# Expert blocks of a mixture layer: the next block's rows are transposed behind the down products, and their first half signals on its own

## The chip, the cores and the metric

The kernel runs on one core of a Trainium2 chip. The metric is the device time of one execution in microseconds, as the median of several runs; lower is better. The engines are TensorE (PE), VectorE (DVE), ScalarE (ACT), GpSimd (POOL) and SyncE (SP). Each has its own instruction queue and works through it in order; they wait for each other by semaphores.

## The reference, cut to what matters

One step of a two-layer decoder for 1024 prompt rows and 8 sample rows of 1024 columns, all in f32. Each layer has a mixer, a layer norm, a mixture of experts and a layer norm. The change lies in the mixture of experts:

```python
vals, idx = lax.top_k(jnp.where(in_group, probs, -1.0), TOP_K)      # 2 of 16 experts for each row
...
for e in range(N_EXPERTS):
    h = jax.nn.silu(xt @ w_gate[e]) * (xt @ w_up[e])                # 1024 -> 256
    y = y + dense_gate[:, e:e + 1] * (h @ w_down[e])                # 256 -> 1024
x = layer_norm(ALPHA * x + f)
```

## The kernel before

`experts` is called once for each of the two layers. It first works out which rows go to which expert and lays them out in half blocks of 64 rows: a half block belongs to one expert. Two half blocks make a block of 128 rows. Then `steps` runs `body(i, u, first)` on every engine for each block j = 2i + u, up to the last one in use. Buffers with index u alternate from block to block.

Of a block, the low half (columns 0 to 63 of the turned rows) is multiplied with weights straight from the ring of four experts' weights (`wgu`, `wd`), and the high half with a copy of its expert's weights (`half_wgu`, `half_wd`, both in `x_rows`), which VectorE and ScalarE make anew for each block. The two products of a pair run in the two column halves of TensorE's array.

The engines' orders in `body` for block j:

- **TensorE.** Waits for the turned rows' two halves (`xca`, `xcv`) and for both parts of the copied gate/up weights (`b_gate_up` at 2j + 2). Gate/up products for k = 0 to 7 (L2432, L2433) into bank 2 + u. Then `transpose_x`: eight transposes (L2405) of the rows of block j + 1 into banks 0 and 1, signal `xt` after the last. Then `down` of block j - 1 (L2417, L2418) into banks 5 and 6. Then two transposes (L2447) of block j's hidden into bank 4, signal `ht`. In the first block of a stage there are no down products.
- **VectorE.** `second_half(j + 1, ..., 0)`: copies part 0 of the gate/up weights of the next block's second half (L2651), once that expert's weights are `loaded` and TensorE is through the fourth gate/up pair (`b_read`). Then the product of silu and up (L2661, signal `h`). Then `copy_x`: the high half of the turned rows out of bank 1 (L2482, signal `xcv`), after `xt`. Then part 1 of the weights (L2651 again, signal `b_gate_up`). Then `out` of block j - 1: y = alpha x + down products (L2645), signal `y`.
- **ScalarE.** `second_half(j - 1)`: down weights of the second half (L2498, `b_down`). Alpha times x (L2507, `alpha_x`). Silu (L2511). `copy_x` of the low half (L2482, `xca`), after `xt`. `out(j - 1)`: store of y by a DMA (L2489), after `y`. Then the copy of the transposed hidden (L2516, `hc`), after `ht`; the down products of block j wait for `hc`.
- **GpSimd.** `load_rows`: the gather of the rows of block j + 1 by an indirect DMA (L2368, L2371), after `xt` and `alpha_x` of the block before.
- **SyncE.** Loads an expert's weights (three DMAs of 1 MB, L2243 and L2245) once the down products of the expert that had the set are through (`halves_plus_1`), waits until they have landed, signals `loaded` (L2347), and goes on to the next expert.

Of the kernel before, what the change touches and what calls it, by code (L numbers as in the profile page):

```python
# [35 lines left out]
P = 128  # L36
# [2220 lines left out]
def experts(nc, io, layer, xr, lg, gates, slots, table, weights, tables, stored, const, ahead, s_ahead):  # L2257
# [7 lines left out]
    with Memory(nc, f"ex{layer}") as m:  # L2265
        wgu, wd, s_w = weights
        p = m.sb("probs", [P, TILES, E])
# [32 lines left out]
        pb = m.psum("pb", [P, 8, 512])  # L2300

        r = {k: m.sem(f"route_{k}") for k in "mx ex as rk chain lanes blocks sum parts part tokens token_list now tokens_set tab".split()}
        q = {k: m.sem(k) for k in "gu xt halves_plus_1 ht silu h xca xcv hc alpha_x y b_read b_gate_up b_down loaded stored".split()}
        s_xs = [m.sem(f"x_rows{u}") for u in range(2)]
        s_st = m.sem("y_rows_stored")
        s_last = m.sem("x_rows_of_last_landed")
# [91 lines left out]
        @block.tensor  # L2398
        def _(pe):
            mm = nc.tensor.matmul  # L2400

            def transpose_x(i, u):
                pe.wait_ge(s_xs[u], 16 * i + 16)
                for k in range(KD):
                    last = nc.tensor.transpose(pb[:, k // 4, P * (k % 4):P * (k % 4) + P], xs[:, u, P * k:P * k + P],  # L2405
                                            const["ident"][:, :])
                last.then_inc(q["xt"], 1)

            def down(j, c):

                w = wd[:, bass.ds(c, 1), :, :].rearrange("p c k n -> p (c k) n")
                pe.wait_ge(q["b_down"], j + 1)
                pe.wait_ge(q["hc"], j + 1)
                for half in range(2):
                    cols = slice(512 * half, 512 * half + 512)
                    for k in range(2):
                        a = mm(pb[0:HALF, 5 + half, :], hT[:, k, 0:HALF], w[:, k, cols], start=(k == 0), stop=(k == 1))  # L2417
                        b = mm(pb[HALF:P, 5 + half, :], hT[:, k, HALF:P], half_wd[:, k, cols], start=(k == 0), stop=(k == 1))  # L2418
                a.then_inc(q["halves_plus_1"], 1)
                b.then_inc(q["halves_plus_1"], 1)  # L2420

            def body(i, u, first):
                j = 2 * i + u
                c = entry(pe, j, 0, E - 1) % SETS
                w = wgu[:, bass.ds(c, 1), :, :].rearrange("p c k n -> p (c k) n")
                pe.wait_ge(q["xca"], j + 1)
                pe.wait_ge(q["xcv"], j + 1)
                pe.wait_ge(q["b_gate_up"], 2 * j + 2)
                if not first:
                    pe.wait_ge(q["h"], j - 1)  # L2430
                for k in range(KD):
                    mm(pb[0:HALF, 2 + u, :], xT[:, k, 0:HALF], w[:, k, :], start=(k == 0), stop=(k == KD - 1))  # L2432
                    last = mm(pb[HALF:P, 2 + u, :], xT[:, k, HALF:P], half_wgu[:, k, :], start=(k == 0), stop=(k == KD - 1))  # L2433
                    if k == 3:
                        last.then_inc(q["b_read"], 1)
                last.then_inc(q["gu"], 1)
                transpose_x(i + u, 1 - u)
                if not (first and u == 0):
                    c_before = entry(pe, j - 1, 0, E - 1) % SETS
                    if not first:  # L2440
                        pe.wait_ge(q["y"], j - 1)
                    down(j - 1, c_before)
                pe.wait_ge(q["h"], j + 1)
                if not (first and u == 0):
                    pe.wait_ge(q["hc"], j)
                for k in range(2):
                    last = nc.tensor.transpose(pb[:, 4, P * k:P * k + P], h[:, u, P * k:P * k + P], const["ident"][:, :])  # L2447
                last.then_inc(q["ht"], 1)
            a = A[:, :, :].rearrange("p t e -> p (t e)")
            pe.wait_ge(tables.sem, tables.all)  # L2450
            keep_busy(nc, pb[:, 1, :], const["ident"], 28)
            pe.wait_ge(r["as"], 1)
            mm(pb[:, 5, 0:TILES * E], t["ones"][:, :], A[:, :, :].rearrange("p t e -> p e t"), start=True, stop=True)
            mm(pb[:, 6, 0:TILES * E], t["not_earlier"][:, :], a, start=True, stop=True).then_inc(r["rk"], 1)
            keep_busy(nc, pb[:, 1, :], const["ident"], 28)
            pe.wait_ge(r["blocks"], 1)
            for c in range(2):
                pe.wait_ge(r["lanes"], c + 1)
                for i in range(TILES):
                    j = TILES * c + i  # L2460
                    g = RW * (j % RG)
                    last = mm(pb[g:g + RW, 7, 0:P], in_block[0:rows(i), c, i, :], at_lane[c][0:rows(i), i, :],
                              start=(j < RG), stop=(j + RG >= 2 * TILES))
            last.then_inc(r["parts"], 1)
            pe.wait_ge(r["sum"], 2)
            pe.wait_ge(r["part"], 1)
            mm(pb[:, 4, 0:NBLK], part, group_sum[:, 0:NBLK], start=True, stop=True).then_inc(r["tokens"], 1)
            transpose_x(0, 0)
            keep_busy(nc, pb[:, 2, :], const["ident"], 24)
            pe.wait_ge(r["tab"], 1)  # L2470

            pe.sem_inc(q["halves_plus_1"], 1)
            final = steps(pe, body)
            c = entry(pe, final, 0, E - 1) % SETS
            pe.wait_ge(q["y"], final)
            down(final, c)

        def copy_x(eng, copy, half, sem, j):

            eng.wait_ge(q["xt"], j + 1)  # L2480

            copy(xT[:, 4 * half:4 * half + 4, :], pb[:, half, :].rearrange("p (k t) -> p k t", k=4)).then_inc(q[sem], 1)  # L2482

        @block.scalar
        def _(act):
            def out(j):

                act.wait_ge(q["y"], j + 1)
                act.dma_start(io["slots_out"][bass.ds(j * P, P), :], y[:, :]).then_inc(s_st, 16)  # L2489

            def second_half(j, first):

                expert = entry(act, T_HALVES + j, 0, E - 1)
                act.wait_ge(q["loaded"], expert + 1)
                if not first:
                    act.wait_ge(q["halves_plus_1"], 2 * j + 1)
                src = wd[:, bass.ds(expert % SETS, 1), :, :].rearrange("p c k n -> p (c k n)")
                nc.scalar.copy(half_wd.rearrange("p k n -> p (k n)"), src).then_inc(q["b_down"], 1)  # L2498

            def body(i, u, first):  # L2500
                j = 2 * i + u
                if not (first and u == 0):
                    second_half(j - 1, first)
                act.wait_ge(s_xs[u], 16 * i + 16)
                if not first:
                    act.wait_ge(q["y"], j - 1)
                nc.scalar.activation(ax[:, u, :], xs[:, u, :], ACT.Identity, scale=ALPHA).then_inc(q["alpha_x"], 1)  # L2507
                act.wait_ge(q["gu"], j + 1)
                if not first:
                    act.wait_ge(q["ht"], j - 1)  # L2510
                nc.scalar.activation(h[:, u, :], pb[:, 2 + u, 0:FF], ACT.Silu).then_inc(q["silu"], 1)  # L2511
                copy_x(act, nc.scalar.copy, 0, "xca", j + 1)
                if not (first and u == 0):
                    out(j - 1)
                act.wait_ge(q["ht"], j + 1)
                nc.scalar.copy(hT[:, :, :], pb[:, 4, 0:2 * P].rearrange("p (k t) -> p k t", k=2)).then_inc(q["hc"], 1)  # L2516
            act.wait_ge(r["mx"], 1)
            nc.scalar.activation(p[:, :, :], p[:, :, :], ACT.Exp).then_inc(r["ex"], 1)
            act.wait_ge(r["parts"], 1)
            nc.scalar.copy(part, pb[0:RG * RW, 7, 0:P]).then_inc(r["part"], 1)  # L2520
            copy_x(act, nc.scalar.copy, 0, "xca", 0)
            act.wait_ge(r["tab"], 1)
            expert = entry(act, T_HALVES, 0, E - 1)
            act.wait_ge(s_stored, n_stored)
            act.wait_ge(q["loaded"], expert + 1)
            nc.scalar.copy(half_wgu[:, 0:4, :].rearrange("p k n -> p (k n)"),
                           wgu[:, bass.ds(expert % SETS, 1), 0:4, :].rearrange("p c k n -> p (c k n)")).then_inc(q["b_gate_up"], 1)
            last = steps(act, body)
            second_half(last, False)
            out(last)  # L2530
            act.wait_ge(s_st, 16 * last + 16)
            act.sem_inc(q["stored"], 1)
# [384 lines left out]
```

## Time and profile before

| what | value |
|---|---|
| median of 3 runs | 1544.02 us (1543.89 to 1549.71) |
| the profiled execution | 1542.83 us |
| its span, first to last instruction | 1541.0 us |
| TensorE busy | 1384.9 us (90%) |
| VectorE busy | 737.4 us (48%) |
| ScalarE busy | 443.1 us (29%) |
| mean granted TensorE clock | 0.943 of full |
| gate/up products (L2432 and L2433 side by side) | 279.8 us |
| down products (L2417 and L2418 side by side) | 148.3 us |

The profile is of one execution. The two expert stages lie at about 787 to 1052 us and 1210 to 1483 us of the span. A busy share is a mean over stages with different limits, so what the change is worth has to be read inside the expert stages. Matmuls are pipelined: the busy times of two that run side by side overlap, and the start of one to the start of the next tells how long a product takes.

### The profile page before, as it was taken

To read this page: it belongs to the slowest core of one execution; us is meant where nothing else is said; L and a number is where in the kernel's file an instruction comes from. 1 tells how busy PE (TensorE), PEld (TensorE's weight loads), DVE (VectorE), ACT (ScalarE), POOL (GpSimd) and SP (SyncE) were. 2 spreads that over 40 slices of the span, in tenths; PEclk is the share of its full clock that TensorE was granted. 3 is DMA by queue.
4 is the path that set the end of the run, shared out by engine and by line. 5 is a ranking of instruction groups with operands and counts; after the bars stand their busy time and mean duration, and the time that the engine had idled before them with its cause. 6 is when DMAs were issued, how large, how long until landed. Compare 5 with 4: busy or idle time off the path is not lost. (4 is left out here: it accounts for less than half of the span.)

```text
span 1541.0 us, 28066 instructions
## 1 busy us (share of the span) xinstructions
PE 1384.9 (90%) x11029; PEld 812.2 (53%) x11030; DVE 737.4 (48%) x1097; ACT 443.1 (29%) x804; POOL 209.9 (14%) x257
## 2 busy tenths in 40 slices
PE   6999999998789988999879999973998799999856
PEld 4666666665688874555553333322797533333212
DVE  1004444467467753867543333333884433333218
ACT  1004456432323321211113333321321223333311
POOL 4000000000434412110000110104100000100031
PEclk8999999999799998999989999995998899999978
DMA  8593000000300013000477788874204777886445
GB/s 216 98 368 90 2 28 28 28 1 4 72 20 4 5 31 121 28 28 29 166 269 249 276 299 292 283 237 163 97 21 176 271 251 254 287 305 241 175 163 207
DMA packets 135338, 226.76 MB, mean 147 GB/s; under 512 B 21970, under 2 KB 100803, under 8 KB 134954
## 3 DMA queue, kind: packets, MB, share of 16 engines
q1 hardware_dynamic: 114434, 151.13, 30.6%
q0 software_dynamic: 15184, 53.67, 9.5%
q10 hardware_dynamic: 5616, 20.45, 3.3%
q8 instruction: 79, 1.29, 0.3%
q14 instruction: 25, 0.20, 0.0%
HBM read 176.42 MB, written 50.35 MB: 147 GB/s over the span
## 5 line engine op out<-in xcount | busy, mean ns | idle before, releaser
L2432 PE MATMUL ex_pb<-ew_w_gate_up,ex_xT 128*64 x624 | 279.8, 602 | 7.8 <-DVE x_rows L2651 7.8
L2433 PE MATMUL ex_pb<-x_rows,ex_xT 128*64 128x512 f32 x624 | 279.8, 602 | 0.0
L518 PE MATMUL pj_pb<-pj_xT,pj_w 128*128 128x348 f32 (+1 forms) x912 | 275.5, 458 | 0.8 <-ACT pj_xT L553 0.8
L518 PEld LDWEIGHTS pj_pb<-pj_xT,pj_w 128*128 128x128 f32 x912 | 170.1, 189 | 94.7 <-issue 5.7
L2651 DVE COPY x_rows<-ew_w_gate_up 128x2048 f32 x80 | 97.8, 1222 | 174.6 <-PE ex_pb L2433 90.2
L2432 PEld LDWEIGHTS ex_pb<-ew_w_gate_up,ex_xT 128*64 128x64 f32 x624 | 83.1, 138 | 173.4 <-issue 173.1
L2417 PE MATMUL ex_pb<-ew_w_down,ex_hiddenT 128*64 x312 | 148.3, 620 | 11.8 <-ACT x_rows L2498 11.8
L2418 PE MATMUL ex_pb<-x_rows,ex_hiddenT 128*64 128x512 f32 x312 | 148.3, 620 | 0.0
L2417 PEld LDWEIGHTS ex_pb<-ew_w_down,ex_hiddenT 128*64 128x64 f32 x312 | 40.8, 141 | 89.1 <-issue 89.1
L2498 ACT COPY x_rows<-ew_w_down 128x2048 f32 x39 | 74.1, 1899 | 31.8 <-issue 29.6
L2433 PEld LDWEIGHTS ex_pb<-x_rows,ex_xT 128*64 128x64 f32 x624 | 83.1, 138 | 0.0
L829 DVE SCALAR_TENSOR_TENSOR mixed<-pj_pb,v_mu,mixed 128x347 f32<-128x347 f32 (+1 forms) x42 | 24.0, 572 | 106.4 <-ACT mixed L674 106.3
L2645 DVE TENSOR_TENSOR ex_y_rows<-ex_x_rows,ex_pb 128x1024 f32<-128x1024 f32 x37 | 45.1, 1220 | 61.8 <-PE ex_pb L2418 61.8
L2516 ACT COPY ex_hiddenT<-ex_pb 128x256 f32<-128x256 f32 x39 | 14.5, 373 | 197.2 <-DVE ex_y_rows L2645 197.2
L2368 POOL COPY ex_tokens_now<-ex_token_of_slot 128x1 uint32 (+1 forms) x41 | 10.1, 247 | 438.9 <-ACT ex_x_rows L2507 389.1
L674 ACT ACTIVATE mixed<-pj_pb,pj_one_minus_mu 128x347 f32<-128x347 f32 (+1 forms) x42 | 23.0, 548 | 149.0 <-PE pj_pb L518 149.0
L2004 PE MATMUL mo_pb<-late_rows,projected_qkv 128*128 128x512 f32 x128 | 60.3, 615 | 0.0
L2405 PEld LDWEIGHTS ex_pb<-k_ident,ex_x_rows 128*128 128x128 f32 x328 | 36.6, 145 | 43.4 <-issue 31.6
L2004 PE MATMUL mo_pb<-mo_w,minus_kk_then_y 128*128 128x512 f32 x128 | 58.0, 593 | 0.0
L2405 PE MATMUL ex_pb<-k_ident,ex_x_rows 128*128 128x128 f32 x328 | 46.6, 287 | 11.5 <-DMA ex_x_rows<-scratch_x_stored,ex_tokens_now 11.5
L2661 DVE TENSOR_TENSOR ex_hidden<-ex_hidden,ex_pb 128x256 f32<-128x256 f32 x39 | 16.4, 420 | 73.2 <-ACT ex_hidden L2511 73.2
L2733 PE MATMUL cb_pb<-cb_expert_rows,cb_gate_diagonals 128*128 128x512 f32 (+1 forms) x72 | 34.2, 623 | 16.0 <-DMA cb_expert_rows<-scratch_slots_out,slots 13.2
(431 smaller groups left out, 2248.6 us busy)
## 6 DMA issues: line engine op xcount, KB each, us to landing
ew_w_gate_up<-in_w_ex_gate SPq DMA_DIRECT2D x32, 1024.0 KB, 6.1
ew_w_gate_up<-in_w_ex_up SPq DMA_DIRECT2D x32, 1024.0 KB, 10.0
ew_w_down<-in_w_ex_down SPq DMA_DIRECT2D x32, 1024.0 KB, 12.5
scratch_slots_out<-ex_y_rows ACTq DMA_DIRECT2D x39, 512.0 KB
scratch_slots_out<-pj_tmp POOLq DMA_DIRECT2D x3, 4096.0 KB, 21.7
scratch_x_stored<-x_rows SPq DMA_DIRECT2D x16, 512.0 KB
pj_w<-in_w_in SPq DMA_DIRECT2D x7, 1024.0 KB, 9.7
minus_kk_then_y<-in_x_prompt SPq DMA_DIRECT2D x8, 512.0 KB, 5.9
```

The costliest lines, as they stand in the source:

```text
L518: last = nc.tensor.matmul(product(at)[:, 0:tn], w[:, k_slab % NW, k, c0:c0 + mrows], xT[:, k, x0:x0 + tn], start=(k == 0), stop=(k == KD - 1))
L829: last = stt(out=out[:, 0:n_prompt], in0=product(at)[:, 0:n_prompt], scalar=mu, in1=out[:, 0:n_prompt], op0=ALU.mult, op1=ALU.add)
L2004: last = mm(pb[0:n, 2 * (i % 2) + h, :], lhs(k, i), (w[:, k, 512 * h:512 * h + 512] if k < 4 else w_swa[:, k - 4, 512 * h:512 * h + 512]), ...
L2405: last = nc.tensor.transpose(pb[:, k // 4, P * (k % 4):P * (k % 4) + P], xs[:, u, P * k:P * k + P], const["ident"][:, :])
L2417: a = mm(pb[0:HALF, 5 + half, :], hT[:, k, 0:HALF], w[:, k, cols], start=(k == 0), stop=(k == 1))
L2418: b = mm(pb[HALF:P, 5 + half, :], hT[:, k, HALF:P], half_wd[:, k, cols], start=(k == 0), stop=(k == 1))
L2432: mm(pb[0:HALF, 2 + u, :], xT[:, k, 0:HALF], w[:, k, :], start=(k == 0), stop=(k == KD - 1))
L2433: last = mm(pb[HALF:P, 2 + u, :], xT[:, k, HALF:P], half_wgu[:, k, :], start=(k == 0), stop=(k == KD - 1))
L2498: nc.scalar.copy(half_wd.rearrange("p k n -> p (k n)"), src).then_inc(q["b_down"], 1)
L2645: nc.vector.tensor_tensor(y[:, :], ax[:, u, :], pb[:, 5:7, :].rearrange("p b n -> p (b n)"), ALU.add)\
L2651: nc.vector.tensor_copy(half_wgu[:, 4 * part:4 * part + 4, :].rearrange("p k n -> p (k n)"), src)\
L2733: last = nc.tensor.matmul(out[0:n, h, :], diag[0:n, i % 2, c, 0:n], r[0:n, i, c, half], start=(c == 0), stop=(c == 1))
```

## The change

Four edits, all in `experts`:

- On TensorE, `transpose_x` for block j + 1 moves from ahead of the down products of block j - 1 to behind them, so it stands right ahead of the transposes of hidden.
- The fourth transpose signals `xt_low`; the eighth signals `xt` as before. ScalarE's copy of the low half waits for `xt_low`, VectorE's of the high half for `xt`.
- On TensorE the wait for the high half (`xcv`) moves from ahead of the gate/up products to ahead of k = 4. The wait for `b_gate_up` stays.
- On ScalarE the copy of the transposed hidden moves ahead of `out(j - 1)`.

```diff
@@ transpose_x
                     last = nc.tensor.transpose(pb[:, k // 4, P * (k % 4):P * (k % 4) + P], xs[:, u, P * k:P * k + P],
                                             const["ident"][:, :])
+                    if k == 3:
+                        last.then_inc(q["xt_low"], 1)
                 last.then_inc(q["xt"], 1)
@@ body of TensorE
                 pe.wait_ge(q["xca"], j + 1)
-                pe.wait_ge(q["xcv"], j + 1)
                 pe.wait_ge(q["b_gate_up"], 2 * j + 2)
                 if not first:
                     pe.wait_ge(q["h"], j - 1)
                 for k in range(KD):
+                    if k == 4:
+                        pe.wait_ge(q["xcv"], j + 1)
...
                 last.then_inc(q["gu"], 1)
-                transpose_x(i + u, 1 - u)
                 if not (first and u == 0):
                     c_before = entry(pe, j - 1, 0, E - 1) % SETS
                     if not first:
                         pe.wait_ge(q["y"], j - 1)
                     down(j - 1, c_before)
+                transpose_x(i + u, 1 - u)
                 pe.wait_ge(q["h"], j + 1)
@@ copy_x
-            eng.wait_ge(q["xt"], j + 1)
+            eng.wait_ge(q["xt" if half else "xt_low"], j + 1)
@@ body of ScalarE
                 copy_x(act, nc.scalar.copy, 0, "xca", j + 1)
+                act.wait_ge(q["ht"], j + 1)
+                nc.scalar.copy(hT[:, :, :], pb[:, 4, 0:2 * P].rearrange("p (k t) -> p k t", k=2)).then_inc(q["hc"], 1)
                 if not (first and u == 0):
                     out(j - 1)
-                act.wait_ge(q["ht"], j + 1)
-                nc.scalar.copy(hT[:, :, :], pb[:, 4, 0:2 * P].rearrange("p (k t) -> p k t", k=2)).then_inc(q["hc"], 1)
```

## Rows read from the trace of the kernel before

**Rows 1.** The page, its costliest groups: one instruction of this line a block.
```profile
L2516 ACT COPY ex_hiddenT<-ex_pb 128x256 f32<-128x256 f32 x39 | 14.5, 373 | 197.2 <-DVE ex_y_rows L2645 197.2
```

**Rows 2.** Busy times by stretch, from a block's first gate/up product to the next's.
```profile
core 0: us, PE busy (x) PEld busy (x) DVE busy (x) ACT busy (x) POOL busy (x), PEclk, DMA share, GB/s
895.50:907.50 12.00, 12.00 (x59) 4.33 (x58) 4.57 (x6) 4.20 (x5) 1.72 (x2) 1.00 0.84 303
907.50:919.90 12.40, 12.08 (x59) 4.33 (x59) 4.76 (x6) 4.20 (x5) 1.15 (x2) 1.00 0.91 311
919.90:933.70 13.80, 12.13 (x58) 4.41 (x58) 4.31 (x6) 4.20 (x5) 1.14 (x2) 1.00 0.82 286
...
811.57:823.56 11.99, 11.99 (x59) 4.41 (x59) 3.70 (x5) 2.80 (x4) 1.14 (x2) 1.00 0.39 137
...
993.70:1011.60 17.90, 12.37 (x59) 4.40 (x58) 4.54 (x6) 4.20 (x5) 1.14 (x2) 0.93 0.80 275
1011.60:1025.70 14.10, 14.08 (x58) 4.83 (x58) 4.52 (x6) 4.20 (x5) 1.68 (x2) 0.85 0.98 303
...
1423.50:1442.80 19.30, 12.39 (x60) 4.43 (x60) 4.76 (x6) 4.20 (x5) 1.15 (x2) 0.91 0.74 259
1442.80:1456.40 13.60, 13.60 (x60) 4.73 (x60) 4.48 (x6) 4.20 (x5) 1.92 (x2) 0.88 0.26 96
```

**Rows 3.** Timeline of TensorE in an undisturbed block: start us, us, engine, line, what.
```profile
902.54 1.09 PE L2405 MATMUL ex_pb<-k_ident,ex_x_rows 128*128 128x128 f32 x8
...
903.56 0.64 PE L2417 MATMUL ex_pb<-ew_w_down,ex_hiddenT 128*64 x1
...
907.15 0.44 PE L2447 MATMUL ex_pb<-k_ident,ex_hidden 128*128 128x128 f32 x2
...
907.51 0.64 PE L2432 MATMUL ex_pb<-ew_w_gate_up,ex_xT 128*64 x1
...
914.53 1.09 PE L2405 MATMUL ex_pb<-k_ident,ex_x_rows 128*128 128x128 f32 x8
```

**Rows 4.** The same timeline, ScalarE and VectorE beside it.
```profile
903.67 0.59 ACT L2482 COPY ex_xT<-ex_pb 128x512 f32<-128x512 f32 x1 [0.63 <-PE ex_pb L2405]
903.67 0.69 DVE L2482 COPY ex_xT<-ex_pb 128x512 f32<-128x512 f32 x1 [0.18 <-PE ex_pb L2405]
...
904.28 1.22 DVE L2651 COPY x_rows<-ew_w_gate_up 128x2048 f32 x1
...
907.47 1.22 DVE L2645 TENSOR_TENSOR ex_y_rows<-ex_x_rows,ex_pb 128x1024 f32<-128x1024 f32 x1 [1.98 <-PE ex_pb L2418]
...
909.24 0.37 ACT L2516 COPY ex_hiddenT<-ex_pb 128x256 f32<-128x256 f32 x1 [4.99 <-DVE ex_y_rows L2645]
```

**Rows 5.** Timeline, end of a stage's first block, which has no down products.
```profile
808.32 1.09 PE L2405 MATMUL ex_pb<-k_ident,ex_x_rows 128*128 128x128 f32 x8
...
809.33 0.44 PE L2447 MATMUL ex_pb<-k_ident,ex_hidden 128*128 128x128 f32 x2
...
809.45 0.69 DVE L2482 COPY ex_xT<-ex_pb 128x512 f32<-128x512 f32 x1 [0.18 <-PE ex_pb L2405]
...
810.05 1.22 DVE L2651 COPY x_rows<-ew_w_gate_up 128x2048 f32 x1
...
811.57 0.64 PE L2432 MATMUL ex_pb<-ew_w_gate_up,ex_xT 128*64 x1 [1.80 <-DVE x_rows L2651]
```

**Rows 6.** Timelines of SyncE's queue and VectorE: the last expert's weights, both stages.
```profile
993.61 0.38 SPq L2243 DMA_DIRECT2D ew_w_gate_up<-in_w_ex_gate  x1
...
1008.13 1.23 DVE L2651 COPY x_rows<-ew_w_gate_up 128x2048 f32 x1 [13.36 <-SPq L2347]
...
1423.39 0.38 SPq L2243 DMA_DIRECT2D ew_w_gate_up<-in_w_ex_gate  x1
...
1439.22 1.23 DVE L2651 COPY x_rows<-ew_w_gate_up 128x2048 f32 x1 [14.54 <-SPq L2347]
```

**Rows 7.** Timeline, end of the first expert stage.
```profile
1037.60 1.22 DVE L2645 TENSOR_TENSOR ex_y_rows<-ex_x_rows,ex_pb 128x1024 f32<-128x1024 f32 x1 [1.89 <-PE ex_pb L2418]
...
1043.96 1.11 PE L2417 MATMUL ex_pb<-ew_w_down,ex_hiddenT 128*64 x1 [6.16 <-ACT x_rows L2498]
```

More of the change, by code:

```diff
@@ L2302, in experts @@
         r = {k: m.sem(f"route_{k}") for k in "mx ex as rk chain lanes blocks sum parts part tokens token_list now tokens_set tab".split()}
-        q = {k: m.sem(k) for k in "gu xt halves_plus_1 ht silu h xca xcv hc alpha_x y b_read b_gate_up b_down loaded stored".split()}
+        q = {k: m.sem(k) for k in "gu xt_low xt halves_plus_1 ht silu h xca xcv hc alpha_x y b_read b_gate_up b_down loaded stored".split()}
         s_xs = [m.sem(f"x_rows{u}") for u in range(2)]
```

## Prediction

> **What bounds the kernel now.** I read the page first: the list of costliest groups says that the expert blocks are 39 in all, over the two expert stages [rows 1]. Then the table of stretches, one stretch a block, counted from the first gate/up product of a block to that of the next [rows 2]. The reader should see two kinds of row. In an undisturbed one (895.50 to 907.50) TensorE is busy for 12.00 of 12.00 us at granted clock 1.00, with VectorE at 4.57 and ScalarE at 4.20: the block is bound by TensorE and nothing else is near it. In the others TensorE was kept waiting, or ran at a lower clock.
>
> Third, the order on TensorE inside an undisturbed block [rows 3]. Gate/up at 907.51, transposes of the next rows at 914.53: 7.02 us for gate/up. The down products start 1.02 us after the transposes (902.54 to 903.56), the transposes of hidden 3.59 us after that (907.15), and the next gate/up 0.36 us later. 7.02 + 1.02 + 3.59 + 0.36 = 11.99 us. TensorE has no hole in it.
>
> Fourth, what the other engines do meanwhile [rows 4]. Both halves of the turned rows are copied at 903.67, 1.13 us after the transposes began. VectorE then copies the second part of the second half's gate/up weights (L2651, 904.28, 1.22 us), which ends at 905.50. The next gate/up needs the rows and both weight parts: `b_gate_up` is awaited in full at the top of the block. All of that is there at 905.50 and wanted at 907.51. The cover is the down products, and the spare time is 2.0 us.
>
> **The change part by part.** *The move of the eight transposes.* It removes no instruction. The down products now follow gate/up directly; I take 7.02 us for gate/up, as the wait, the table entry and the products replace the transposes at the same place, then 3.59 us to the end of the down products. Then come the transposes, at time T, and behind them only the transposes of hidden, 0.36 us, instead of 3.59 + 0.36.
>
> What is late next is VectorE's program order, which the diff leaves alone: copy of the high half of the turned rows (waits for all eight transposes), then L2651 (second weight part), then the next gate/up can start. The low half's own signal doesn't help this chain, nor does the later `xcv` wait on TensorE, since `b_gate_up` stays where it was and its second increment comes behind the high copy.
>
> The trace of before has exactly this order once per stage, in the first block, which has no down products [rows 5]: transposes at 808.32, hidden's at 809.33, VectorE's copy at 809.45, L2651 at 810.05, gate/up at 811.57 after 1.80 us of idle that is put down to L2651. From the transposes to gate/up: 3.25 us. I take it as it stands.
>
> New block: 7.02 + 3.59 + 3.25 = 13.86 us against 11.99: **+1.87 us a block**. It holds for each step from one gate/up to the next in which down products stood between: not for the first step of a stage, which had this order already. 39 blocks in two stages make 37 steps, less 2 is 35. 35 x 1.87 = **+65.4 us**, all of it on TensorE's path.
>
> *The signal after the fourth transpose.* ScalarE's copy of the low half can start earlier than 1.13 us after T. Nobody who is last waits for it: 0. The cover is VectorE's chain; without that, see the second rival. The extra increment and the wait for `xcv` ahead of the fifth product don't show in this trace. Bounds: 0 below (no data leaves the path), and above 0.1 us each, since a table entry and three waits between hidden's transposes and gate/up fit into 0.36 us together with two transposes [rows 3]; I take 0, the nearer to that row, and keep 35 x 0.1 = 3.5 us for the range.
>
> *ScalarE: hidden's copy ahead of `out`.* Before, the copy at 909.24 waited behind the store, which waited for y (907.47) [rows 4]. Now it runs at once, and behind it come the store, the down weights' copy and alpha times x. Who waits for it is the down product a whole gate/up later: 0 in the middle of a stage. POOL's queue waits for alpha x and the transposes; the rows it fetches are wanted a block later than they land, and that point moves later: 0. The store's DMA is issued some 2.5 us later in the block, in a block that grows by 1.87: 0.
>
> *y, and the tail of a stage.* VectorE's y (L2645) stands behind L2651. In the last block nothing covers this: y, store, down weights' copy, last down products. Before, y started at 1037.60 and the last down products at 1043.96, 6.36 us later [rows 7]; gate/up had begun at 1025.70 [rows 2], so 18.26 us in all. Now y starts when VectorE is through L2651: T + 1.73 for its start (808.32 to 810.05) and 1.13 for the following one, T + 2.86, with T 10.61 us after gate/up; then 6.36, less 0.39 for the hidden copy that no longer stands in between. 10.61 + 2.86 + 6.36 - 0.39 = 19.44: +1.2 us, twice: **+2.4 us**.
>
> *Waits for weights that go.* Six steps were longer than 11.99 us [rows 2]: 12.40, 13.80, 17.90, 14.10 (clock 0.85), 19.30, 13.60 (clock 0.88). Together 91.1 - 71.9 = 19.2 us lost. Two rows show the cause of the big ones [rows 6]: the last expert's load is issued at 993.61, when the down products free a set, and VectorE starts on it at 1008.13, 14.5 us later; in the second stage 1423.39 and 1439.22, 15.8 us. The issue stood 0.1 us ahead of gate/up; now the down products end 3.25 us ahead of gate/up, and the issue comes some 2.9 us ahead of it. The weights are there 11.6 and 12.9 us into the block, and gate/up follows 3.5 us after them as before (1008.13 to 1011.60): 15.1 and 16.4 us against 13.86, so 1.2 and 2.5 us remain. The two small waits (0.4 and 1.8 us) are shorter than what one block gives to the loads, and go. That TensorE ran at a lower clock came only with the two longest idles (17.90 less 12.37 and 19.30 less 12.39 us, so 5.5 and 6.9 us); what remains is 3.1 and 4.4 us with the 1.9 us, in pieces, so I let the cost of the clock go as well. **-(19.2 - 1.2 - 2.5) = -15.5 us**. If none of it comes back, 0; if all, -19.2.
>
> **Sum**, against the profiled execution's 1542.83 us: +65.4 + 2.4 - 15.5 = +52.3, 1595.1 us. The profiled run lies 1.2 us under the median of the runs (1544.02), so I say **1596 us** for a median, +3.4%.
>
> **Rivals.** *The clock falls in every block.* Each block now has about 1.9 us of idle TensorE. In the two steps at low clock, 2.1 and 1.6 us were lost [rows 2]; at 35 blocks x 1.85 that is +65 more, 1661 us. Against it: the same 1.80 us of idle stands ahead of 811.57 and the stretch behind it reads 1.00; the stretch of 13.80 us, with 1.7 us idle, reads 1.00 too [rows 2, 5]. For it: it would now recur every 13.9 us, which no row shows. Chance 5%. The Trainium skill, page "TensorE: Matmul & The Clock Gate", section "A second HAM failure mode: psum-queue depth-cycling", describes this: frequent short idles between groups of products make the clock go back and forth between its two levels.
>
> *The copies are all that is exposed, and the loads pay for it.* This is the case on the other side, not slower. It needs the second weight part to be in place ahead of the turned rows, or TensorE not to stand still for `b_gate_up`. Then gate/up waits for the low copy alone: fourth transpose done some 0.62 us after T (a little over half of the 1.09 us of the eight), 0.63 for ScalarE's copy, 0.30 from copy to product as at 811.27 to 811.57: T + 1.55 against T + 1.37, +0.18 us a block, 6.3 us. With the sets freed 1 us earlier, 5 to 9 of the 19.2 us come back: 1540 to 1544 (1542.8 + 6.3 + 1.2, less that). It decides at whether the 1.22 us copy of L2651 stands behind the high copy in VectorE's order; the code says so, and [rows 5] shows TensorE waiting for it. Chance 4%: 3% within half a per cent, 1% faster.
>
> *The price is paid, but no wait for weights shrinks*, because the late loads come from their own succession and not from the set's release: 1542.8 + 65.4 + 2.4 + 1.2 = 1612 us. For it: in the first stage the loads run back to back for long stretches. Against it: then 35 us more time would help them even more. Chance 15%.
>
> **How the numbers follow.** Forecast with its neighbourhood, 76%: 1587 to 1606 (0.1 us a block either way, 3.7 us of loads either way, 2.4 of tail). Rival without recovery 15%, clock 5%, covered 4%. The range for 8 in 10 goes from 1582 to 1614: it takes in the third rival, and for its lower end a block that costs 1.6 us instead of 1.87 with all 19.2 us given back (1542.8 + 56 + 2.4 - 19.2 + 1.2 = 1583). What measurement can tell from no change is about 0.5%, 8 us. Slower by over that: 96%; within: 3%; faster: 1%.
>
> **What would show it.** TensorE's gate/up group (L2432) gets an idle of about 1.9 us in 37 of 39 blocks, released by VectorE's L2651, some 65 us in total instead of 7.8; undisturbed blocks last 13.86 us; VectorE's high copy is released by the transposes and L2651 follows it by 0.6 us; the wait at the last expert's load shrinks from about 5.6 us to under 3; the clock in the middle of a stage stays 1.00. Wrong would be: gate/up released by ScalarE's copy or by nothing, a block near 12.2 us, or stretches well under 1.00.

## The result

| | before | after |
|---|---|---|
| median of the runs shown together | 1545.8 us (4 runs) | 1595.71 us (4 runs, 1594.8 to 1598.55) |
| ratio | | 1.0312, 95% interval 1.0273 to 1.0350 |
| profiled execution / its span | 1542.83 / 1541.0 us | 1598.55 / 1596.7 us |

The change makes the kernel slower by 3.1%. 1596 us was forecast, and 3.4% on the median then known.

The timeline of the changed kernel, one block in the middle of the first expert stage, is below (start us, us, engine, line, what). Its file has more lines, so the numbers have moved, and they move again in the kernels of the experiments: here L2419 are the down products, L2435 gate/up, L2450 hidden's transposes, L2485 the copies of the turned rows, L2654 the weights' copy, L2648 y.

```profile
902.93 0.59 PE L2419 MATMUL ex_pb<-ew_w_down,ex_hiddenT 128*64 x1
...
906.47 1.09 PE L2405 MATMUL ex_pb<-k_ident,ex_x_rows 128*128 128x128 f32 x8
907.16 0.59 ACT L2485 COPY ex_xT<-ex_pb 128x512 f32<-128x512 f32 x1 [3.63 <-PE ex_pb L2405]
...
907.40 0.38 PE L2450 MATMUL ex_pb<-k_ident,ex_hidden 128*128 128x128 f32 x2
907.60 0.69 DVE L2485 COPY ex_xT<-ex_pb 128x512 f32<-128x512 f32 x1 [3.62 <-PE ex_pb L2405]
...
908.21 1.22 DVE L2654 COPY x_rows<-ew_w_gate_up 128x2048 f32 x1
909.34 1.22 DVE L2648 TENSOR_TENSOR ex_y_rows<-ex_x_rows,ex_pb 128x1024 f32<-128x1024 f32 x1
909.71 0.64 PE L2435 MATMUL ex_pb<-ew_w_gate_up,ex_xT 128*64 x1 [1.93 <-DVE x_rows L2654]
...
916.62 0.59 PE L2419 MATMUL ex_pb<-ew_w_down,ex_hiddenT 128*64 x1
```

This is [rows 5] in every block. ScalarE's low half is copied by 907.75, VectorE's high half by 908.29, and gate/up still waits until L2654 is through at 909.43. In [rows 3, 4] the same copies ran under the down products. From gate/up to down products 6.91 us, to the transposes 3.54, to gate/up 3.24.

The waits of TensorE (us in total, times, longest), and the stretches from one gate/up to the next, columns as in [rows 2]:

```profile
PE ex_pb L2435 <- DVE x_rows L2654: 69.1, 37, 1.9
```

```profile
841.44:855.13 13.69, 11.76 (x59) 4.55 (x59) 4.69 (x6) 4.20 (x5) 1.14 (x2) 1.00 0.79 279
855.13:868.73 13.60, 11.76 (x58) 4.55 (x59) 4.52 (x6) 4.20 (x5) 1.14 (x2) 1.00 0.35 105
...
1480.33:1494.98 14.65, 11.98 (x59) 4.54 (x59) 4.51 (x6) 4.20 (x5) 1.15 (x2) 1.00 0.91 310
1494.98:1508.58 13.60, 11.76 (x58) 4.53 (x59) 4.51 (x6) 4.20 (x5) 1.15 (x2) 1.00 0.27 100
```

That is 69.1 us of waiting in 37 starts; before it was 7.8 us in 6. TensorE works 11.76 us of a block's 13.60 or 13.69; the two lengths alternate, 13.65 in the mean. The only block longer than that is the one at 1480.33, so of the six long stretches of [rows 2] one small one is left.

The next table shows where the 55.7 us between the two spans lie. The edges are the first gate/up product of an expert stage and the start of its last down products:

| stretch | before | after | difference |
|---|---|---|---|
| up to the first gate/up product | 801.3 | 803.9 | +2.6 |
| first expert stage | 242.7 | 262.3 | +19.6 |
| between the expert stages | 177.4 | 185.6 | +8.2 |
| second expert stage | 252.7 | 276.8 | +24.1 |
| to the end | 67.0 | 68.2 | +1.2 |

So 43.7 us are in the expert stages, and 12 outside them, where the change touches nothing. Most of those are one thing. In both traces TensorE stands still for 19.9 us behind the first expert stage, does 8.4 us of small products for the layer's mixer and stands still for 2.0 us more. The stretches below start behind that, first before, then after. The products come in the same order in both; at the lower clock fewer of them fit into a stretch.

```profile
1080.90:1085.00 4.10, 4.05 (x19) 3.50 (x20) 3.97 (x5) 0.43 (x1) 2.68 (x3) 0.60 1.01 393
1085.00:1090.00 5.00, 5.00 (x22) 1.36 (x22) 1.45 (x2) 1.81 (x3) 0.00 (x0) 1.00 0.72 285
```

```profile
1101.90:1106.00 4.10, 4.09 (x17) 3.58 (x18) 3.93 (x5) 0.27 (x1) 2.65 (x3) 0.50 1.02 399
1106.00:1111.00 5.00, 5.00 (x12) 0.85 (x10) 1.45 (x2) 1.97 (x3) 0.00 (x0) 0.50 0.59 234
...
1121.00:1126.00 5.00, 5.00 (x19) 4.55 (x19) 4.86 (x8) 2.24 (x3) 0.00 (x0) 0.50 0.00 0
1126.00:1131.00 5.00, 5.00 (x20) 3.94 (x19) 0.47 (x1) 0.00 (x0) 0.00 (x0) 0.82 0.00 0
```

Before, TensorE's clock is back at 1.00 (2.4 GHz) at 1085; after, it stays at 0.50 (1.2 GHz) until some 1128, with TensorE busy all the time from 1106 on. The profiles of this case take 175 to 179 us between the stages, or 184 to 186, and nothing between. A median of any kernel here can hold these 8 us or not, which has to be kept in mind below. The kernel before, run again beside the experiments, shows a split of like size: 43 of its 59 runs took 1539.4 to 1548.3 us, 16 took 1552.1 to 1560.1, and none lies between.

### The profile page after: what moved, and what is told of

Same layout as the page of the kernel before. It is cut to its first block and busy times, and to the rows that moved or that the text cites. A ratio compares the mean times of both kernels' runs of the same rounds, so it can differ in the third digit from the quotient of the medians.

```text
span 1596.7 us, 28031 instructions
## 1 busy us (share of the span) xinstructions
PE 1384.8 (87%) x11029; PEld 825.3 (52%) x11030; DVE 735.2 (46%) x1097; ACT 443.2 (28%) x804; POOL 204.8 (13%) x257
## 5 line engine op out<-in xcount | busy, mean ns | idle before, releaser
L2435 PE MATMUL ex_pb<-ew_w_gate_up,ex_xT 128*64 x624 | 276.0, 595 | 69.1 <-DVE x_rows L2654 69.1
L2436 PE MATMUL ex_pb<-x_rows,ex_xT 128*64 128x512 f32 x624 | 276.1, 595 | 0.0
L2435 PEld LDWEIGHTS ex_pb<-ew_w_gate_up,ex_xT 128*64 128x64 f32 x624 | 82.3, 137 | 231.2 <-issue 230.9
L2654 DVE COPY x_rows<-ew_w_gate_up 128x2048 f32 x80 | 97.8, 1223 | 143.5 <-PE ex_pb L2436 123.6
L2419 PE MATMUL ex_pb<-ew_w_down,ex_hiddenT 128*64 x312 | 144.9, 608 | 16.4 <-ACT x_rows L2501 16.4
L2420 PE MATMUL ex_pb<-x_rows,ex_hiddenT 128*64 128x512 f32 x312 | 144.8, 608 | 0.0
L2419 PEld LDWEIGHTS ex_pb<-ew_w_down,ex_hiddenT 128*64 128x64 f32 x312 | 43.7, 141 | 106.6 <-issue 106.6
L2485 DVE COPY ex_xT<-ex_pb 128x512 f32<-128x512 f32 x41 | 28.4, 692 | 135.6 <-PE ex_pb L2405 135.6
L2485 ACT COPY ex_xT<-ex_pb 128x512 f32<-128x512 f32 x41 | 24.0, 586 | 150.1 <-PE ex_pb L2405 150.1
```

What stands on the lines that cost most here:

```text
L2654: nc.vector.tensor_copy(half_wgu[:, 4 * part:4 * part + 4, :].rearrange("p k n -> p (k n)"), src)\
```

## The experiments

Theory A is the forecast's: VectorE's order, high copy and then second weight part, sets the start of gate/up, and nothing else of the change is on the path. The table gives what the timelines of the profiled executions show for all kernels: the undisturbed block, the two expert stages together, the stretch between them, and then the medians with the kernel before beside them on the same chip.

```
kernel             block     expert stages  between  median    before
before             11.99     495.4          177.4    1545.8
after              13.65     539.1          185.6    1595.71   1545.8
e1_move_only       13.65     541.4          185.2    1597.88   1545.9
e2_wait_at_k4      12.12     498.4          185.9    1554.76   1545.9
e3_weights_first   12.12     489.5          176.7    1548.13   1545.9
e9_middle_warm     13.65     538.1          175.3    1587.55   1545.9
e4_before_longer   11.99     500.8          185.0    1556.79   1543.98
e5_after_longer    14.24     581.4          177.0    1628.05   1543.98
e6_before_k4       11.99     491.0          177.0    1549.07   1543.98
e10_k4_warm        11.99     489.9          184.3    1546.61   1543.98
e13_after_dense    13.65     539.0          179.0    1590.50   1544.44
e12_k4_dense       11.99     490.5          177.4    1541.78   1544.44
e14_both_dense     12.12     492.4          177.5    1541.87   1544.44
```

**One part of the change alone: `e1_move_only`.**

```diff
--- before
+++ e1_move_only
                 last.then_inc(q["gu"], 1)
-                transpose_x(i + u, 1 - u)
...
                     down(j - 1, c_before)
+                transpose_x(i + u, 1 - u)
                 pe.wait_ge(q["h"], j + 1)
```

> The kernel before with one part of the change: the eight transposes stand behind the down products; no signal after the fourth, both waits at the top of gate/up, hidden's copy behind the store as before. Theory A (VectorE's chain of high copy and second weight part sets the start of gate/up; all else is off the path): a block of 13.65 us and a total within 3 us of the changed kernel, 1593 to 1599. Theory B (the split signal or hidden's earlier copy takes part in the time, either way): more than 5 us away from the changed kernel.

Measured: 1597.88 us, ratio to before 1.0308 (1.024 to 1.0377), block 13.65 us. Its waits:

```profile
PE ex_pb L2432 <- DVE x_rows L2651: 69.2, 37, 2.0
```

These are the same 69 us of wait in the same 37 places. The move is the whole price; the early signal, the later wait for the high half and hidden's earlier copy neither cost nor bring anything that shows in the medians. The expert stages take 2.3 us more than in the changed kernel, nearly all in the last two steps of the second (15.15 and 15.30 us against 14.65 and 13.60). There the clock fell once, for 1.7 us:

```profile
1494.97:1510.27 15.30, 13.46 (x58) 4.96 (x59) 4.51 (x6) 4.20 (x5) 2.04 (x2) 0.89 0.24 87
```

TensorE had stood still twice within 3.6 us ahead of it, 1.65 us ahead of hidden's transposes and 1.53 ahead of gate/up. In the same place of the changed kernel it stood still for 1.14 and 1.52 us, and the clock stayed at 1.00.

**The wait for the second weight part at its first user: `e2_wait_at_k4`.**

```diff
--- after
+++ e2_wait_at_k4
-                pe.wait_ge(q["b_gate_up"], 2 * j + 2)
+                pe.wait_ge(q["b_gate_up"], 2 if first and u == 0 else 2 * j + 1)
...
                     if k == 4:
                         pe.wait_ge(q["xcv"], j + 1)
+                        pe.wait_ge(q["b_gate_up"], 2 * j + 2)
```

> The changed kernel, with TensorE's wait for the second weight part moved from the top of gate/up to ahead of k = 4, its first user. Nothing is left out of the work. Theory A: gate/up starts when ScalarE's low copy is done, some 1.5 us behind the transposes instead of 3.24, and the fifth pair, 1.7 us later, finds the second part just there: a block of 12.0 to 12.2 us, most of the waits for late weights come back (5 to 15 us), in all 1540 to 1555. Theory B (TensorE's own order or the exposed copies of the turned rows are the price): the block stays above 13 us and the total above 1580.

Measured: 1554.76 us (1.0036, 1.0008 to 1.0063), at the upper end of what theory A gave. Timeline:

```profile
896.09 1.09 PE L2405 MATMUL ex_pb<-k_ident,ex_x_rows 128*128 128x128 f32 x8
896.79 0.58 ACT L2486 COPY ex_xT<-ex_pb 128x512 f32<-128x512 f32 x1 [3.63 <-PE ex_pb L2405]
...
897.22 0.69 DVE L2486 COPY ex_xT<-ex_pb 128x512 f32<-128x512 f32 x1 [3.62 <-PE ex_pb L2405]
...
897.75 0.64 PE L2436 MATMUL ex_pb<-ew_w_gate_up,ex_xT 128*64 x1 [0.35 <-ACT ex_xT L2486]
...
897.83 1.22 DVE L2655 COPY x_rows<-ew_w_gate_up 128x2048 f32 x1
```

Gate/up starts 1.66 us behind the transposes, released by ScalarE's low copy, 0.08 us before L2655 even starts. So 1.53 us of a block's 1.66 are gone with one wait moved. Here the early signal comes to use: the low copy starts 0.70 us behind the first transpose, where [rows 3, 4] have 1.13, and gate/up now waits for it. The waits for late weights, though, are back (16.50 and 18.86 us for the two longest blocks), and all ten runs lie between 1552.4 and 1557.9: the profile has the long stretch between the stages, 185.9 us.

**The order on VectorE turned: `e3_weights_first`.**

```diff
--- after
+++ e3_weights_first
-                copy_x(dve, nc.vector.tensor_copy, 1, "xcv", j + 1)
                 dve.wait_ge(q["gu"], j + 1)
                 second_half(j + 1, expert, 1)
+                copy_x(dve, nc.vector.tensor_copy, 1, "xcv", j + 1)
```

> The changed kernel, with VectorE's order turned: second weight part first (during the down products), then the high copy. All waits on TensorE as in the changed kernel. Theory A: L2651's 1.2 us falls under the down products; gate/up starts at the low copy, 1.5 us behind the transposes, the high copy is done 1.8 us behind them and wanted at 3.2: a block of 12.0 us, in all 1538 to 1552. Theory B: no change against the changed kernel, above 1580.

Measured: 1548.13 us (0.9996, 0.9962 to 1.0031): no loss is left that can be told from noise, and TensorE's program is untouched. Timeline:

```profile
894.25 1.22 DVE L2654 COPY x_rows<-ew_w_gate_up 128x2048 f32 x1
...
896.82 1.09 PE L2405 MATMUL ex_pb<-k_ident,ex_x_rows 128*128 128x128 f32 x8
...
897.51 0.59 ACT L2485 COPY ex_xT<-ex_pb 128x512 f32<-128x512 f32 x1 [3.63 <-PE ex_pb L2405]
...
897.95 0.69 DVE L2485 COPY ex_xT<-ex_pb 128x512 f32<-128x512 f32 x1 [2.48 <-PE ex_pb L2405]
...
898.48 0.64 PE L2435 MATMUL ex_pb<-ew_w_gate_up,ex_xT 128*64 x1 [0.35 <-ACT ex_xT L2485]
```

VectorE now idles 2.48 us ahead of the high copy instead of 3.62: the 1.2 us weights' copy has moved under the down products. The block is 12.12 us, 0.13 over before: the exposed low copy, which the second rival priced at 0.18. The expert stages take 8.9 us less than those of `e2_wait_at_k4`: 3.5 us in the two tails (18.26 and 18.17 us from the last gate/up to the last down products, against 19.99 and 19.95), the rest mostly in steps with late weights (14.44 and 16.96 us for the longest two). The profile is that of the fastest of ten runs (1538.91 to 1554.06).

**The same chain made longer: `e4_before_longer` and `e5_after_longer`.** The edit is one and the same in both, a copy ahead of the second weight part that nobody needs:

```diff
                 src = wgu[:, bass.ds(expert % SETS, 1), 4 * part:4 * part + 4, :].rearrange("p c k n -> p (c k n)")
+                if part == 1:
+                    nc.vector.tensor_copy(pb[:, 7, :], src[:, 0:2 * FF])
```

> The kernel before with one more VectorE copy in each block, right ahead of L2651's second part: 512 columns of the weights into an unused PSUM bank, some 0.5 us, 37 times behind down-product blocks. Nothing else changes. Theory A: 2.0 us are to spare there, so the block stays 12.0 us and the total stays as before but for blocks whose weights come late (5 of them, 0.5 us each): 0 to +5 us. Theory B (VectorE's chain isn't what counts): 0 as well.

> The changed kernel with the same added copy. Theory A: the whole of it, some 0.5 us, stands in each block between the high copy and the gate/up product: block 13.65 plus its length, 37 times, in all 15 to 25 us over the changed kernel. Theory B: 0 to 3 us.

In before the block stays at 11.99 us, in the changed kernel it grows to 14.24, by the 0.60 us from the added copy's start to L2656's:

```profile
884.46 0.68 DVE L2655 COPY ex_pb<-ew_w_gate_up 128x512 f32 x1
885.06 1.22 DVE L2656 COPY x_rows<-ew_w_gate_up 128x2048 f32 x1
...
886.56 0.64 PE L2435 MATMUL ex_pb<-ew_w_gate_up,ex_xT 128*64 x1 [2.52 <-DVE x_rows L2656]
```

So theory A holds for the block, but both totals missed what was expected of them. `e4_before_longer` was to cost 0 to 5 us and cost 12.8 (1556.79, ratio 1.0070, 1.0042 to 1.0099). In its profile the expert stages cost 5.4, of which 1.2 are the two first blocks and nearly all the rest blocks with late weights; the stretch between the stages costs 7.6 more, 185.0 us against 177.4, the clock again. `e5_after_longer` was to cost 15 to 25 us over the changed kernel and cost 32 (1628.05, two runs), though its stretch between the stages is short. 12 of its 37 steps took 15.9 to 16.0 us instead of 14.2 to 14.3. Below are first two stretches of such a step, behind the idle of 2.52 us above, and then one of a step behind 2.43 us in which the clock stayed:

```profile
886.50:889.50 3.00, 2.94 (x10) 1.11 (x12) 0.90 (x1) 0.40 (x1) 0.00 (x0) 0.65 1.09 358
889.50:892.50 3.00, 3.00 (x12) 0.85 (x10) 0.28 (x1) 2.46 (x2) 0.18 (x1) 0.78 1.07 371
...
872.20:875.20 3.00, 2.93 (x14) 1.09 (x16) 1.01 (x1) 0.54 (x1) 0.00 (x0) 1.00 1.08 360
```

That is the forecast's first rival, the clock falling inside the loop, in a third of the blocks and at 1.7 us each where 1.85 were put down. Which of the two idles stood ahead doesn't decide it: six of the falls come behind 2.43 us and six behind 2.52. With the 1.52 to 1.93 us of idle of the changed kernel it happens in none of 37 steps, with 2.40 to 2.52 us in 12 of 37, 20 us in all. A further 37 x 0.59 = 21.8 us is what the copy itself costs; the two make up the 42.3 us by which the expert stages grew (1.0 more in the tails and 1.0 less in the block at 1480.33 cancel).

**Only the waits moved, on the kernel before: `e6_before_k4`.**

```diff
--- before
+++ e6_before_k4
-                pe.wait_ge(q["xcv"], j + 1)
-                pe.wait_ge(q["b_gate_up"], 2 * j + 2)
+                pe.wait_ge(q["b_gate_up"], 2 if first and u == 0 else 2 * j + 1)
...
                 for k in range(KD):
+                    if k == 4:
+                        pe.wait_ge(q["xcv"], j + 1)
+                        pe.wait_ge(q["b_gate_up"], 2 * j + 2)
```

> The kernel before, with only the waits moved: high half of the turned rows and second weight part are awaited ahead of k = 4. Undisturbed blocks have nothing to gain (all there 2.0 us early). Theory A: the first block of each stage gives back up to 1.8 us, each of the five gate/up starts that waited for late weights up to 1.7 us: 4 to 10 us less than before, 1536 to 1542. Theory B: the wait inside the products costs 0.1 us in each of 37 blocks or more: no gain or a loss.

Missed as a total: 1549.07 us, ratio 1.0013 (0.9986 to 1.0040), no difference. The expert stages did give 4.4 us in its profile (first blocks 8.94 instead of 10.27), but that is the fastest of ten runs (1540.48 to 1553.45), and 4.4 us are less than the 8 that the clock between the stages can add to a run. The wait inside the products costs nothing that shows: the block is 11.99.

**The clock between the stages: `e9_middle_warm`, `e10_k4_warm`, `e13_after_dense`, `e12_k4_dense`.** The edits, on the changed kernel and on `e6_before_k4`; `e9_middle_warm` and `e10_k4_warm` have 48 matmuls of no use in the first place alone, the dense form has 56 there and the second place besides:

```diff
             pe.wait_ge(pm.sem, pm.all)
+            keep_busy(nc, pb[:, 7, :], const["ident"], 48)
...
                 i = ORDER[j]
+                if j == 1:
+                    keep_busy(nc, pb[:, 7, :], const["ident"], 14)
                 pe.wait_ge(qa["x"], j + 1)
```

> The changed kernel, with 48 matmuls of no use on TensorE between the expert stages, in an idle stretch of some 20 us in which it waits for the first normed rows. In the profile of the changed kernel the clock stays at 0.50 for some 26 us behind this stretch, in that of before it rises at once. Theory C (that is a cost of its own, in most runs of the changed kernel): the clock is 1.00 behind the stretch, and the total is 6 to 12 us less than the changed kernel's, 1584 to 1590. Theory D (it comes and goes from run to run, and the medians hold little of it): less than 4 us between the medians.

> The changed kernel with matmuls of no use between the expert stages, more of them and in two places: 56 in the idle stretch ahead of the first normed rows, 14 in the idle of 2 us behind the first light products. The stretch between the expert stages (last down products to next first gate/up) took 177.4 us in the profile of before and 185.5 in the changed kernel's, the 8 us being clock. Theory C (a lower clock that stays is the 8 us; more work on TensorE keeps it up): 174 to 180 us there and 1585 to 1590 in all, with under 4 us between runs. Theory D (the extra work doesn't decide it): some runs or all near 1596.

Both came near theory C: 1587.55 and 1590.50 us against 1595.71, with 175.3 and 179.0 us between the stages. One of the four runs of the second took 1605.92, which theory C doesn't allow. But these medians were not taken side by side. As ratios to the kernel before, they are 1.0249 (1.0182 to 1.0316) and 1.0335 (1.0278 to 1.0392), and both intervals hold the 1.0312 of the changed kernel. So the shorter stretch is seen in the two profiles, and a shorter total is not shown.

> The kernel of e6_before_k4 with the 48 matmuls of no use of e9_middle_warm. Runs of before fall into two groups, near 1544 and near 1554 us. Theory C (the second group is the clock that stays at its lower level behind the idle stretch between the expert stages): all runs lie close together, at or under the faster group of e6_before_k4, 1532 to 1542, and the spread is under 5 us. Theory D: the spread of some 10 us stays.

> The kernel of e6_before_k4 with the extra matmuls of e13_after_dense. Theory C: runs within 5 us of each other, 1534 to 1542, faster than before by 3 to 9 us. Theory D: the 10 us spread of e6_before_k4 and e10_k4_warm stays.

Here theory C failed: `e10_k4_warm` had 184.3 us between the stages, and its runs spread from 1538.37 to 1550.63; `e12_k4_dense` from 1536.41 to 1548.01. The added matmuls don't prevent the long stretch. Whether they make it rarer isn't shown: it is in one of the five profiles with them and in four of the eight without. In the profile of `e12_k4_dense` the clock falls again behind them, with TensorE busy for 8.86 and then 10.00 of ten microseconds:

```profile
1070.00:1080.00 10.00, 8.86 (x67) 8.51 (x66) 9.34 (x12) 2.75 (x4) 8.17 (x7) 0.93 0.95 331
1080.00:1090.00 10.00, 10.00 (x49) 9.78 (x49) 4.92 (x7) 1.44 (x3) 7.59 (x8) 0.56 0.95 344
```

**The best of both: `e14_both_dense`,** the changed kernel with the edits of `e2_wait_at_k4`, `e3_weights_first` and `e13_after_dense`.

> The changed kernel with both cures, TensorE's wait for the second weight part ahead of k = 4 and VectorE's copy of it ahead of the high copy, and the extra matmuls of e13_after_dense. Theory A: what is left of the change is the exposed low copy, a block of 12.1 us against before's 11.99 (+4 us over 35), and the waits for late weights shrink since the sets come free earlier; in all 1532 to 1542. If the exposed copy costs more than theory A says, the block is over 12.3 us and the total above 1545.

Measured: 1541.87 us, ratio 0.9986 (0.9954 to 1.0018), block 12.12 us. `e12_k4_dense` stands at 0.9972 (0.9942 to 1.0002). They lie 2.6 and 2.7 us under before, and neither interval excludes no change.

## Why the forecast held

**The mechanism.** Right, and shown from four sides: the part alone gives the whole loss, either of two edits that take the second weight part out of the chain takes the loss away, and a copy put into the chain costs its length after and nothing before. The row that carried it was the first block of a stage [rows 5], which had the new order already.

**The price of a block.** The forecast was 1.87 us and the measured price 1.66, so 58.0 us over 35 steps instead of 65.4. Three terms were each a little high. Gate/up ahead of the down products takes 6.91 us and not 7.02: I took the 7.02 from a stretch that ended in transposes. The down products take 3.54 and not 3.59. From the transposes to gate/up it is 3.24 and 3.15 in turn, and not 3.25 each time. Put otherwise, TensorE stands still for 1.84 or 1.93 us a block, and gets 0.23 back, since its own work takes 11.76 us and not 11.99.

**The waits for weights.** 15.5 us of 19.2 were to come back, and 18.2 did: the six stretches of [rows 2] are gone but for one that is 1.0 us too long. The first stage keeps nothing, where 1.2 us were expected. The term that was mis-sized is the landing of the last load, which I had put at the same 14.5 and 15.8 us behind its issue. The issue did come 2.9 us ahead of gate/up, as forecast, but VectorE starts on the weights 12.8 and 14.0 us behind it (1015.92 to 1028.68, and in the second stage):

```profile
1477.43 0.38 SPq L2243 DMA_DIRECT2D ew_w_gate_up<-in_w_ex_gate  x1
...
1491.40 1.23 DVE L2654 COPY x_rows<-ew_w_gate_up 128x2048 f32 x1 [10.14 <-SPq L2347]
```

That is 11.1 us into the block (1480.33 to 1491.40) instead of 12.9. Why the loads took less was not tried; the transfers have 1.66 us more a block. That the third rival (no recovery) fell is certain: it needed the 19.2 us of waits to stay, and 1.0 is left.

**The tail of a stage.** The forecast was +1.2 us for each, and +1.8 and +2.3 were measured (19.99 and 19.94 us against 18.23 and 17.68 from the last gate/up to the last down products). The step that failed is the -0.39 us for hidden's copy. It doesn't come off. In before ScalarE's down weights' copy started 3.05 us behind the end of y with hidden's copy in between; now it starts 3.36 us behind it (1060.71 to 1064.07) with only the store's issue in between, which stands there in both, in time that the profile puts down to issue:

```profile
1064.07 1.90 ACT L2501 COPY x_rows<-ew_w_down 128x2048 f32 x1 [5.72 <-issue]
1066.16 1.11 PE L2419 MATMUL ex_pb<-ew_w_down,ex_hiddenT 128*64 x1 [8.22 <-ACT x_rows L2501]
```

And for the second stage I took the tail of the first (18.26 us in the forecast, 18.23 by the timeline), where it had been 17.68.

**The total.** 58.0 - 18.2 + 4.0 = 43.8 us in the expert stages, where 52.3 were forecast. That the median hit 1596 within 0.3 us is luck: the 8.5 us that the expert stages fell short by are more than made up by the 8 us between the stages, which the forecast didn't have, and by 4 us elsewhere, and the profiled execution lies 2.8 us over its kernel's median. With a short stretch in between and matmuls of no use added, the changed kernel takes 1587.55 us (`e9_middle_warm`), inside the range all the same. All four runs of the changed kernel lie within 4 us of each other (1594.8 to 1598.55), as if all had the long stretch; whether the change makes it likelier, and so costs these 8 us too, stays open. The other 4 us, ahead of the first expert stage and at the end, are no more than executions differ by: these two stretches take 801.3 to 809.5 and 66.2 to 68.7 us in the 13 profiles, with the same code in them.

**The rivals.** The clock in every block: no stretch of the changed kernel in the middle of a stage is under 1.00, so this rival was wrong, but by a margin of 0.6 us of idle, as `e5_after_longer` shows. The Trainium skill, "TensorE: Matmul & The Clock Gate", "A second HAM failure mode: psum-queue depth-cycling", tells of a kernel in which frequent short idles make the clock swing. The trace of `e5_after_longer` agrees with it (12 falls in 37 steps), that of the changed kernel does not (none). The covered case is what `e3_weights_first` does: 0.13 us a block where 0.18 were worked out, some 9 of the 19.2 us back where 5 to 9 were. It is decided where the forecast put it, at the place of L2651 in VectorE's order. (The forecast's sum for it, 1542.8 + 6.3 + 1.2 less 5 to 9, is 1541 to 1545 and not 1540 to 1544.)

## What to carry to other kernels

When a step is moved to just ahead of its user, follow the whole queue of the engine that copies its result out: what stands behind the copy and is awaited together with it is exposed too, and here that was 1.5 us of the 1.66. Look for a first or last iteration in which the moved order already occurs; its rows give the price. And await each part at its first user: one wait moved four pairs of products later gave back as much a block as the order of the copies did, 1.53 us.

## What the runs showed of the hardware

- A repeated idle of TensorE of 1.52 to 1.93 us a block left the clock at 1.00 in 37 of 37 steps of the changed kernel; in `e1_move_only` it fell in one of 37, where two idles of 1.65 and 1.53 us stood close together. 2.40 to 2.52 us (`e5_after_longer`) let it fall in 12 of 37, for 1.7 us each.
- Behind 19.9 us of idle, 8.4 us of small products and 2.0 us more of idle, the clock came back within 5 us in the profile of before and after some 26 us in that of the changed kernel, with the same products and TensorE busy: 8 us of a total. Matmuls of no use in the idle did not secure the first case (184.3 us between the stages in `e10_k4_warm`); what decides stays open.
- Down products that follow gate/up directly start 0.43 us behind the last pair; transposes there started 0.53 us behind it, and the product behind transposes then took 0.64 instead of 0.59 us.
